# Routed experts of one encoder layer: tokens gathered by an indirect transfer instead of by matmuls

## The reference

```python
def route(t, w_router, b_router):
    scores = jax.nn.sigmoid((t @ w_router).astype(jnp.float32))
    choice = scores + b_router.astype(jnp.float32)
    ...                      # the best 4 of 8 groups, in them the best 8 of 64 experts
    w = w / (w.sum(-1, keepdims=True) + 1e-20) * ROUTED_SCALE
    return idx, w

def block(acc, xs):          # tok: tokens of one expert, w: their weights, e: the expert
    tok, w, e = xs
    xb = t[tok]
    yb = (jax.nn.silu(xb @ w_gate[e]) * (xb @ w_up[e])) @ w_down[e]
    return acc.at[tok].add((yb * w[:, None]).astype(acc.dtype)), None
```

## Time and profile before

| | us |
|---|---|
| median of 3 runs | 933.45 (931.59 to 934.66) |
| the profiled execution | 933.76 |
| its span in the trace | 932.0 |

### The profile page before, as it was taken

One profiled execution on the slowest core, in us unless ns is written; L12 is line 12 of the kernel. 1 busy time (PEld: TensorE's weight loads), 2 busy tenths in 40 slices (PEclk: granted clock), 3 DMA queues, 4 the chain that ended last, 5 costly groups with the idle time before them and its releaser, 6 DMA issues.

```text
span 932.0 us, 13868 instructions
## 1 busy us (share of the span) xinstructions
PE 846.4 (91%) x4404; PEld 464.1 (50%) x4405; DVE 273.5 (29%) x801; ACT 247.9 (27%) x484; POOL 88.4 (9%) x189
## 2 busy tenths in 40 slices
PE   7699999697889899999999999999999999999920
PEld 3199983534686744444454444444444444444500
DVE  2354426435225611121211121211211112121138
ACT  2353424134113312121222212122221212121321
POOL 3000011200022000101101010110101011010100
PEclk9889989798798999999999999999999999999965
DMA  8934447452526368099995999699996999999183
GB/s 325 362 135 160 180 181 276 151 181 92 228 80 257 111 272 366 40 375 417 426 426 242 405 426 427 261 390 419 427 421 249 404 423 427 425 427 427 57 326 131
DMA packets 55370, 273.83 MB, mean 294 GB/s; under 512 B 12720, under 2 KB 13056, under 8 KB 27312
## 3 DMA queue, kind: packets, MB, share of 16 engines
q1 hardware_dynamic: 41728, 257.05, 67.8%
q0 software_dynamic: 6560, 12.55, 3.6%
q10 hardware_dynamic: 7056, 3.88, 1.4%
HBM read 261.34 MB, written 22.07 MB: 304 GB/s over the span
## 4 chain that ended last, share of the span: by engine, by line
PE 82%; DVE 6%; DMA 6%; ACTq 2%; issue 2%; ACT 1%; SPq 1%; POOL 0%; POOLq 0%; DVEq 0%
PE psum L1174 26%; PE psum L1193 13%; PE psum L1150 9%; PE psum L870 8%; DMA expert_w<-in_w_exp_down 5%; PE psum L1157 4%; PE psum L1071 4%; PE psum L840 3%; DVE y_rank L1627 2%; PE psum L1099 2%; PE psum L1166 1%; PE psum L1089 1%; ACTq L475 1%; PE psum L1183 1%; PE psum L825 1%
## 5 line engine op out<-in xcount | busy, mean ns | idle before, releaser
L1174 PE MATMUL psum<-expert_w,xg 128*64 128x512 f32 x1184 | 263.9, 598 | 3.6 <-DMA expert_w<-in_w_exp_down 2.0
L1174 PEld LDWEIGHTS psum<-expert_w,xg 128*64 128x64 f32 x1184 | 85.7, 137 | 150.4 <-issue 149.8
L1193 PE MATMUL psum<-expert_w,hidT 128*64 128x512 f32 x592 | 135.2, 598 | 0.0
L1150 PE MATMUL psum<-h2hl,sel 128*128 128x512 f32 x380 | 97.8, 403 | 0.5 <-ACT acc L611 0.5
L1150 PEld LDWEIGHTS psum<-h2hl,sel 128*128 128x128 f32 x380 | 68.4, 188 | 43.7 <-issue 30.0
L629 ACT ACTIVATE silg<-psum 128x256 f32<-128x256 f32 x37 | 14.2, 384 | 261.1 <-PE psum L1174 261.1
L1589 DVE SCALAR_TENSOR_TENSOR hid<-psum,ws,silg 128x256 f32<-128x256 f32 x37 | 17.9, 484 | 195.9 <-ACT silg L629 195.9
L1193 PEld LDWEIGHTS psum<-expert_w,hidT 128*64 128x64 f32 x592 | 39.2, 136 | 69.6 <-issue 69.6
L1599 DVE COPY y_slot<-psum 128x512 f32<-128x512 f32 x37 | 25.6, 692 | 117.5 <-PE psum L1193 117.5
L618 ACT COPY xs<-psum 128x512 f32<-128x512 f32 x76 | 44.5, 586 | 58.1 <-PE psum L1150 58.1
L1157 PE MATMUL psum<-ident,xs 128*128 128x128 f32 x304 | 47.7, 279 | 0.5 <-ACT xs L618 0.2
(11 more groups left out here) (364 smaller groups left out, 831.5 us busy)
## 6 DMA issues: line engine op xcount, KB each, us to landing
expert_w<-in_w_exp_gate SPq DMA_DIRECT2D x64, 1024.0 KB, 12.8
expert_w<-in_w_exp_up SPq DMA_DIRECT2D x64, 1024.0 KB, 15.1
expert_w<-in_w_exp_down SPq DMA_DIRECT2D x64, 1024.0 KB, 12.7
ring<-in_w_ada SPq DMA_DIRECT2D x24, 1024.0 KB, 7.2
pair<-in_w_in SPq DMA_DIRECT2D x6, 2048.0 KB, 9.5
y_rank<-y_d SPq DMA_DIRECT2D x8, 1024.0 KB, 13.9
pair<-in_w_out SPq DMA_DIRECT2D x2, 2048.0 KB, 8.1
x_tok<-in_x_prompt SPq DMA_DIRECT2D x2, 512.0 KB, 3.8
```

What stands on the lines that cost most here:

```text
L1150: last = mm(bank[q][:, :], sel[:, t // 2, :, :], h2hl[:, t, 4 * q:4 * q + 4, :], start=t == 0, stop=t == 4)
L1174: last = mm(bank[3][CAP * x:CAP * x + CAP, :].rearrange("p (g n) -> p g n", g=2), xg[:, k, CAP * x:CAP * x + CAP], expert_w[2 * u + x][:, ...
L1193: last = mm(bank[4 + half][CAP * x:CAP * x + CAP, :], hidT[:, i, CAP * x:CAP * x + CAP], expert_w[2 * u + x][:, 2, o:o + 512], start=i == ...
```

## The change

The gathered tokens of a block no longer come from ten matmuls. The tokens h2_tok are written to HBM once (h2_d, by ACT's queue), and POOL fetches the 128 rows of a block into xs by an indirect transfer with the token numbers tok (128 slots; those beyond the last token are not moved). h2hl, its low part, the copies to xs and ten matmuls a block go. Slots are chosen three blocks ahead (AHEAD = 3), which needs a table with the pair and the first position for each block: two small matmuls by way of pair_col, between chunks of the shared expert's down. The slots' values are kept for all blocks in slotv. The copy hidT goes from ACT to DVE. POOL's loop holds gather n+2 and scatter n. At the kernel's beginning the small vectors are issued from POOL's queue instead of ACT's, DVE makes two of the four first copies of ada_row, and the first piece of w_in is loaded in two halves.

```diff
@@ -409,7 +420,11 @@
...
-            sp.dma_start(dst, src).then_inc(ring_in[slots_of[n][0]], 16)
+            if n == FIRST_WIN:
+                for q in range(2):
+                    sp.dma_start(dst[:, :, 256 * q:256 * q + 256], src[:, :, 256 * q:256 * q + 256]).then_inc(ring_in[slots_of[n][q]], 16)
+            else:
+                sp.dma_start(dst, src).then_inc(ring_in[slots_of[n][0]], 16)
@@ -469,12 +484,6 @@
-        with nc.allow_non_contiguous_dma(reason="vectors of a few hundred elements"):
-            for dst, src in small[3:]:
-                act.dma_start(dst, src).then_inc(s["small_in"], 16)
-        act.dma_start(pastf[:, :, :], cache_fox_logf[0, 0].rearrange("(j p) h -> p j h", p=P)).then_inc(s["cache_in"], 16)
-        for c in range(2):
-            act.dma_start(states[:, 4, c, :], state_gla[0, 0, 2 * c:2 * c + 2].rearrange("h k v -> (h k) v")).then_inc(s["state_in"], 16)
@@ -482,14 +491,17 @@
...
-            for j in range(4):
+            for j in range(4 if r else 2):
                 act.copy(ada_row[32 * j:32 * j + 2, :], bank[b][32 * j:32 * j + 2, :]).then_inc(s["ada_row"], 1)
...
-            piece_in(act, FIRST_WIN + g // 2)
+            if g == 1:
+                act.wait_ge(ring_in[slots_of[FIRST_WIN][1]], 16 * second_turn)
@@ -603,39 +615,29 @@
...
-            if q == 4:
-                act.wait_ge(s["iota_ok"], 5)
-            act.copy(h2hl[0:TN[i], 2 * i, 4 * (q % 2):4 * (q % 2) + 4, :], bank[4 + q % 2][0:TN[i], :].rearrange("t (k p) -> t k p", k=4)).then_inc(s["h2hi_ok"], 1)
+            act.copy(h2_tok[0:TN[i], i, 512 * (q % 2):512 * (q % 2) + 512], bank[4 + q % 2][0:TN[i], :]).then_inc(s["h2tok_ok"], 1)
+            if q % 2:
+                act.wait_ge(s["h2tok_ok"], q + 1)
+                act.dma_start(h2_d[T0[i]:T0[i] + TN[i]], h2_tok[0:TN[i], i, :]).then_inc(s["h2_out"], 16)
...
-        def slots_in(n):
...
-                act.wait_ge(s["xs_ps"], num(act, n * 2 + (q + 1)))
-                act.copy(xs[:, 4 * q:4 * q + 4, :], bank[q][:, :].rearrange("p (k n) -> p k n", k=4)).then_inc(s["xs_ok"], 1)
...
-            slots_in(n + 1)
-            act.wait_ge(s["hidT_ps"], num(act, n + 1))
-            act.copy(hidT[:, :, :], bank[6][:, 0:2 * P].rearrange("p (j n) -> p j n", j=2)).then_inc(s["hidT_ok"], 1)
             gathered(n + 1)
@@ -687,14 +689,20 @@
...
+        pool.memset(ada_row[:, :], 0.0).then_inc(s["row_zeros"], 1)
+        pool.wait_ge(s["row_zeros"], 1)
+        with nc.allow_non_contiguous_dma(reason="vectors of a few hundred elements"):
+            for dst, src in small[3:]:
+                pool.dma_start(dst, src).then_inc(s["small_in"], 16)
+            pool.dma_start(pastf[:, :, :], cache_fox_logf[0, 0].rearrange("(j p) h -> p j h", p=P)).then_inc(s["state_in"], 16)
+        for c in range(2):
+            pool.dma_start(states[:, 4, c, :], state_gla[0, 0, 2 * c:2 * c + 2].rearrange("h k v -> (h k) v")).then_inc(s["state_in"], 16)
...
-        pool.memset(ada_row[:, :], 0.0).then_inc(s["row_zeros"], 1)
@@ -790,27 +797,53 @@
...
+        def gather(n, mark):
+            ready, free = num(pool, n + 2), num(pool, n * 2)
+            pool.wait_ge(s["tok_ok"], ready)
+            if not isinstance(n, int) or n:
+                pool.wait_ge(s["xg_ps"], free)
+            pool.tensor_tensor(seen[:, mark:mark + 1], zero[:, :], zero[:, :], ALU.add).then_inc(s["g_go"], 1)
+            pool.indirect_dma_start(xs[:, :, :].rearrange("s k p -> s (k p)"), None, h2_d[:, :],
+                                    bass.IndirectOffsetOnAxis(ap=tok[:, 0:1], axis=0), bounds_check=N - 1, oob_is_err=False).then_inc(s["g_in"], 16)
+        def scatter(n):
+            rows_at, halves_at, gone_at = num(pool, n + 2), num(pool, n + 1), num(pool, n * 16 + 16)
+            pool.wait_ge(s["row_ok"], rows_at)
+            pool.wait_ge(s["y_act"], halves_at)
+            pool.wait_ge(s["y_dve"], halves_at)
+            pool.tensor_tensor(seen[:, 1:2], zero[:, :], zero[:, :], ALU.add)
+            pool.indirect_dma_start(y_d[:, :], bass.IndirectOffsetOnAxis(ap=row[:, 0:1], axis=0), y_slot[:, :], None,
+                                    bounds_check=TOPK * N - 1, oob_is_err=False).then_inc(s["y_out"], 16)
+            pool.wait_ge(s["y_out"], gone_at)
+            pool.tensor_tensor(seen[:, 2:3], zero[:, :], zero[:, :], ALU.add).then_inc(s["y_gone"], 1)
+        pool.wait_ge(s["h2_out"], 48)
+        gather(0, 3)
...
+        gather(1, 4)
...
-        with pool.Fori(0, total_blocks(pool)) as n:
...
+        total = total_blocks(pool)
+        with pool.Fori(0, num(pool, total - 2)) as n:
+            gather(n + 2, 5)
+            pool.wait_ge(s["g_go"], num(pool, n + 3))
+            scatter(n)
+        pool.wait_ge(s["xg_ps"], num(pool, total * 2))
...
+        pool.dma_start(xs[:, :, :].rearrange("s k p -> s (k p)"), h2_d[0:P]).then_inc(s["g_in"], 16)
+        scatter(total - 2)
+        scatter(total - 1)
+        pool.tensor_tensor(seen[:, 7:8], zero[:, :], zero[:, :], ALU.add).then_inc(s["y_rows"], 1)
@@ -1132,42 +1166,52 @@
...
-        down(SHARED, lambda k: pe.wait_ge(s["acc_ok"], k - 1) if k >= 2 else None)
-        pe.wait_ge(s["acc_ok"], KC)
-        pe.wait_ge(s["iota_ok"], 5)
-        pe.wait_ge(s["table_ok"], 1)
...
-            for t in range(5):
-                last = mm(bank[q][:, :], sel[:, t // 2, :, :], h2hl[:, t, 4 * q:4 * q + 4, :], start=t == 0, stop=t == 4)
...
-            pe.wait_ge(s["row_ok"], num(pe, n + 1))
+            if not isinstance(n, int) or n:
+                pe.wait_ge(s["slot_ok"], num(pe, n))
             for i in range(3):
...
             last.then_inc(s["slots_ps"], 1)
...
+        down(SHARED, wait_acc, range(1))
+        slot_values(0)
+        down(SHARED, wait_acc, range(1, 6))
+        pe.wait_ge(s["pairs_ok"], 1)
+        mm(bank[4][:, 0:PAIRS], ones[0:1, :], first_f[:, :], start=True, stop=True).then_inc(s["pairs_ps"], 1)
+        down(SHARED, wait_acc, range(6, 7))
+        pe.wait_ge(s["pairs_ok"], 2)
+        mm(bank[4][0:1, 128:256], pair_col[:, 0:1], ident[:, :], start=True, stop=True)
+        mm(bank[4][0:1, 256:384], pair_col[:, 1:2], ident[:, :], start=True, stop=True).then_inc(s["pairs_ps"], 1)
+        down(SHARED, wait_acc, range(7, 8))
+        def gather_T(n):
+            pe.wait_ge(s["g_in"], num(pe, n * 16 + 16))
+            for q in range(2):
+                for k in range(4):
+                    last = tr(bank[q][:, P * k:P * k + P], xs[:, 4 * q + k, :], ident[:, :])
+                last.then_inc(s["xg_ps"], 1)
@@ -1176,14 +1220,12 @@
...
             last.then_inc(s["pgu_ps"], 1)
-            gather(n + 1, 0)
-            gather(n + 1, 1)
+            gather_T(n + 1)
             pe.wait_ge(s["hid_ok"], num(pe, n + 1))
...
-            gather_T(n + 1, 0)
-            gather_T(n + 1, 1)
+            slot_values(n + AHEAD)
             pe.wait_ge(s["hidT_ok"], num(pe, n + 1))
@@ -1194,16 +1236,17 @@
...
-        for q in range(2):
-            gather(0, q)
-        for q in range(2):
-            gather_T(0, q)
+        gather_T(0)
+        slot_values(1)
+        slot_values(2)
+        pe.wait_ge(s["acc_ok"], KC)
+        pe.wait_ge(s["table_ok"], 1)
@@ -1252,6 +1295,10 @@
...
+        dve.wait_ge(s["w_used"], KC)
+        dve.wait_ge(s["row_zeros"], 1)
+        for j in (2, 3):
+            dve.tensor_copy(ada_row[32 * j:32 * j + 2, :], bank[5][32 * j:32 * j + 2, :]).then_inc(s["ada_row"], 1)
@@ -1462,16 +1509,6 @@
...
-        def low_part(q):
@@ -1544,64 +1576,95 @@
...
+        def select_pair(at, e):
+            for x in range(2):
+                dve.tensor_tensor(sel[:, :, x, :], iota[:, bass.ds(at, CAP)].unsqueeze(1).broadcast_to([P, 3, CAP]),
+                                  posm[:, :, bass.ds(e[x], 1)].broadcast_to([P, 3, CAP]), ALU.is_equal)
+                last = dve.tensor_copy(wp[:, :, :, x:x + 1], w_hl[:, :, :, bass.ds(e[x], 1)].bitcast(F32))
+            last.then_inc(s["sel_ok"], 1)
+        def select_slots(n):
+            p = dve.value_load(table[0:1, bass.ds(num(dve, n + 2 * PAIRS + E), 1)], min_val=0, max_val=PAIRS - 1)
+            at = dve.value_load(table[0:1, bass.ds(num(dve, n + (2 * PAIRS + E + MOST)), 1)], min_val=0, max_val=(MAXB + AHEAD - 1) * CAP)
+            e = [expert_at(dve, p * 2 + x, E - 1) for x in range(2)]
+            select_pair(at, e)
+        def slot_columns(n):
+            dve.wait_ge(s["slots_ps"], num(dve, n + 1))
+            at = num(dve, n * 3)
+            for x in range(2):
+                p = slice(CAP * x, CAP * x + CAP)
+                dve.tensor_reduce(slotv[p, bass.ds(at, 2)], bank[2][p, x:8:2].rearrange("p (g m) -> p g m", m=2), AX, ALU.add)
+                last = dve.tensor_copy(slotv[p, bass.ds(num(dve, at + 2), 1)], bank[2][p, 4 + x:5 + x])
+            last.then_inc(s["slot_ok"], 1)
+        def token_rows(n):
+            dve.wait_ge(s["slot_ok"], num(dve, n + 1))
+            if not isinstance(n, int) or n:
```

(36 more changed lines are left out.)

152 lines of the change are left out of this document (61 added, 91 removed).

## The result

The kernel after takes 948.69 us (median of 4 runs, 945.21 to 952.57), the kernel before 933.29 beside it (931.59 to 934.66): ratio 1.0174, 95% interval 1.0147 to 1.0202. The forecast was 925.5 with a range that ended at 942, so both the sign and the range were wrong. The profiled execution of after took 947.37 us, its span is 945.6.

The account below looks back on a forecast made before the run. The expert loop was taken as PE-bound, with 49 us of DMA slack and DMA setting the last pairs. Loop and its start -3.6, front -4.6, tail 0 to +0.3: total -8.2 on 933.8 gives 925.5 us, range 909 to 942.

Parts of the forecast that it names:

- the 3.6 that I had set aside for the clock: Expert loop: half of 7.0 us, the price of PE's clock falling in first blocks after two-block pairs and the last block.
- Part 2: Expert weight loading: the gather adds 0.255 MB a block to DMA; single-block pairs become DMA-bound at 16.1 us a pair.
- the low bound: Expert loop, least time of a pair: 6.29 + 0.51 MB at 426 GB/s, 15.96 us.
- The sign that I had named: Expert loop, trace of after: DMA near 425 GB/s with gaps of about 5 us.
- high bound of 16.5: Expert loop, longest time of a pair: today's 15.9 us plus 0.255 MB at 410 GB/s.
- the rival that began at 16.3: Expert loop: DMA binds at 16.5 us a pair, clock price counts in full; 939 us (934 to 943), chance 0.16.
- the rule of shared engines: DMA: SP, ACT and POOL queues share the same 16 engines and interleave; a further queue saves only issue time.
- Part 1: Expert blocks on PE: without gather matmuls a block takes 13.2 us instead of 14.86 where weights are there.
- Part 3: POOL's gather and scatter: landing 7.8 us, 12.1 us a block, hidden while landing stays under 11.8 in a DMA-bound pair.
- The rival in which the ring binds: POOL's gather and scatter: landing of 11 us gives 15.3 us a block in all 37, about 947 us; chance 0.10.
- Part 4: Start of the expert loop: added table and slot selection steps start block 0 5.7 us later (bounds +3 and +9).
- Part 5: Kernel's beginning: small vectors on POOL's queue and w_in's first load in halves save 4.6 us (bounds 0 and -6).

Follow-up runs that it names:

- the spread slots: Kernel after with each block's slots numbered so that groups of four partitions are filled in turn: 938.66 us, ratio 1.0063.
- the run with the transposes: Kernel after with 24 small extra transposes on PE behind the last block of each pair: 958.76 us, ratio 1.0278.
- its part alone: Kernel before with small vectors on POOL's queue, ada_row copied by ACT and DVE, and the first w_in piece in halves: 928.52 us, ratio 0.9954.

## Why the prediction was wrong, step by step

Predicted span 925.5 - 1.8 = 923.7, measured 945.6: 21.9 us too low. By the terms of the sum: the loads of pair 4 start 3.1 us later than 396 - 4.6; 28 pairs take 468.0 instead of 450.8, +17.2; three gaps 16.9 instead of 15.3, +1.6; the last block, from the end of the loads to the end of its down matmuls, about 2.6 over 13.5; the tail +0.9; less the 3.6 that I had set aside for the clock. That is 21.8.

**Part 2 failed, by the size of its term: a pair takes 16.71 us, not 16.1.** The mechanism was right: single-block pairs became bound by DMA, and PE waits 62.5 us for weights in 25 blocks. Three errors are in the number, all in the same direction. (1) I read the low bound off 8 us at 426 GB/s and took the 410 of the long stretches to contain dry time that a faster PE would fill. I also read those 8 us as if a scatter were in them, and none is: the rows of the scatter issued at 821.64 us move from 825.8 to 829.0, and there it is 419 GB/s. In after, and in the kernel whose gather moves nothing, the queue always has work, at shares of 0.98 to 1.00, and moves 405 to 415. (The sign that I had named, DMA near 425 GB/s, came out at 407.) The long stretches of the earlier trace rows with their share of 0.98 were the row to take. (2) I added one gather to a pair; six pairs hold seven blocks. (3) I priced the gather by its bytes. It costs more, 3.15 us per MB instead of 2.44: for the 31 blocks of the stretches 24.9 us, where the bytes alone give 19 and the fullest engine's rows (about 170 at 0.159 us, an estimate) give 27. That the fullest engine counts was missing from my mechanism; the spread slots show it. From 15.82 us a pair (443.1 / 28, no gathered rows) 24.9 / 28 = 0.89 goes on top, and 15.82 + 0.89 = 16.71. My high bound of 16.5 lay below the truth, so the rival that began at 16.3 (939 us, chance 0.16) was the right one, and it was too cheap as well. The swizzle rule named above pointed to error (3), although it is stated for full transfers; I had weighed only the rule of shared engines.

**The forecast gain was thin.** By its own terms the pairs got slower, 450.8 us against today's 445.0. What made the sum faster were shorter gaps (15.3 against 25.8), a shorter last block and the front, 8.2 us in all. Spread over 28 pairs that is 0.3 us a pair, so a pair of 16.4 would already have turned the sign. PE's gain of 2.3 us a block turned into a wait for weights; it was worth something only up to pair 4, in the gaps and in the last block.

**Part 1 right, and better than forecast**: 12.55 us a block where weights are there, just under the bounds (12.8 to 14.0 us, forecast 13.2). The gain was real and had nowhere to go.

**Part 3 right**: the landing of the gather is 4.3, 8.0 and 10.0 us (least, median, largest; I took 7.8, between 2.5 and 9.3), so the largest is over the 9.3 of my sign and under the 11.8 that counts, and PE waited 0.4 us for it. That once is at 631 us, behind the three blocks in a row without a wait for weights that start at 584.67: the chain there goes from a scatter through POOL to a gather (issued at 622.08, 9.21 us). The rival in which the ring binds gave 947 us, next to the 948.7 measured; it was the right number by the wrong mechanism, and the beats show it: they follow the loads, and the kernel without gathered rows, with the same ring, is 23.4 us faster.

**Part 4 too small.** Block 0 starts at 330.49, where 328.7 was forecast, although its stream started a little earlier than assumed; from the start of the shared down matmuls it is 9.2 us later than before (25.4 us against 16.2), not 5.7, just past the bound of 9. PE in the timeline of after (idle before it, and what ended that, in brackets):

```profile
327.41 0.80 PE L1182 MATMUL psum<-wp,sel 128*128 128x8 f32 x3 [4.52 <-DVE wp L1592]
330.49 9.68 PE L1218 MATMUL psum<-expert_w,xg 128*64 128x512 f32 x32 [2.27 <-issue]
```

The slot matmuls stand 4.5 us for DVE's choice, and block 0 then takes 9.68 us instead of 8.78.

**The clock: the fall was right, its price isn't settled.** The stretch behind a wait of 4.51 us for weights:

```profile
535.90:540.00 4.10, 4.08 (x10) 1.27 (x12) 0.28 (x2) 0.00 (x0) 0.00 (x0) 0.50 1.03 427
541.00:551.40 10.40, 9.69 (x49) 3.71 (x45) 2.18 (x11) 1.85 (x4) 1.38 (x3) 1.00 1.01 423
```

The granted clock is 0.50, the 1.2 GHz level, and back at 2.4 GHz before the block is over; the gate/up takes 9.37 us instead of 6.87, 2.5 more where I took 1.76. Most of it lies in time in which PE would wait for weights anyhow: in the run with the transposes, which takes it away, the stretches are no shorter. It can count in the last block (9.72 us) and where the chain stays on PE behind a slow gate/up (9.97 us at 568.85, 8.78 at 690.33). Against 6.87 these three are 7.9 us longer together, an estimate from above; I had taken 3.6.

**Part 5 right**: L903's unbroken part starts at 43.65 instead of 48.5, -4.9 (forecast -4.6), and its part alone gives -4.4 us.

**The chances.** 0.63 for faster rested on pair times from 15.7 to 16.1, and the row that spoke against them stood in the same group.

## What to carry to other kernels

Where two resources are within a few per cent of each other, moving work from one to the other is decided by the sum of both terms over the whole loop. So price the receiving one by its slowest long stretch, and don't take a peak of a few microseconds for its rate. Count the work by blocks where it comes by blocks. An indirect transfer that fills only some partitions is priced by the fullest DMA engine and not by its bytes (37.8 against 19.1 us for the same bytes): spread the rows over groups of four partitions in both halves. To learn what a moved transfer costs, run it alone in the old kernel, with its real pattern of rows; a stand-in with another pattern cost twice as much and misled.

## What the runs showed of the hardware

- An indirect read of 64 rows of 4 KB beside a saturated queue costs 37.8 us in 28 pairs in partitions 0 to 63 (482.8 against 445.0 us), and 19.1 in 0 to 31 and 64 to 95 (464.1).
- A direct read of 64 rows costs as much as the badly placed indirect one (43 and 41 us in the kernel's time, against 40), at a DMA share of 0.99. Why it does is open; its partitions, 0 to 63 both times, weren't varied.
- Spread slots raise the sustained rate of this load from 407 to 419 GB/s, above anything that a long stretch of the kernel before had shown (413, from 709.8 to 867.8 us).
- After a wait of 4.51 us for weights the granted clock is at the 1.2 GHz level for some 5 us (535.9 to about 541 us), where the gaps of 0.9 us in the kernel before left it at 2.4.
